# First layer of a two-block transformer kernel: own buffers for the squares, one sum each, queries in own banks, another split and order of the 31 conv taps

## The chip, the core and the metric

The kernel runs on one core of a Trainium2 chip. The metric is the time of one execution on the device in microseconds (us), the median of several runs. A core has TensorE (matrix products, into PSUM), VectorE, ScalarE and GpSimd (elementwise work) and SyncE, which here issues the transfers. Each engine works through its own queue in order; semaphores order the engines against each other.

## The reference

Two blocks of two layers each on 512 tokens of width 1,024, all in float32. What the change touches is the mixer of the first layer and the norms:

```python
def conformer_conv(u, b_glu, w_dw, b_dw, ln_g, ln_b):
    u = u + b_glu
    a, gate = jnp.split(u, 2, axis=-1)
    v = a * jax.nn.sigmoid(gate)
    v = causal_dwconv(v, w_dw, b_dw)          # 31 taps for each of 768 channels
    v = layernorm(v, ln_g, ln_b)
    return jax.nn.silu(v)

# layer 0 of first_block
mem_n = rmsnorm(mem, g_mem)                   # 256 tokens
h = rmsnorm(x, g_mix[0])
mem_k, mem_v = jnp.split(mem_n @ w_mem_kv[0], 2, axis=-1)
p = h @ w_in_a[0]
u, q_mem = p[..., :2 * CONV_CH], p[..., 2 * CONV_CH:]
mix = conformer_conv(u, ...)
mem_o = memory_attention(q_mem, mem_k, mem_v) # 4 heads of 64, 256 keys
x = x + jnp.concatenate([mix, mem_o], axis=-1) @ w_out[0]
x = x + conv_ffn(rmsnorm(x, g_ffn[0]), ...)
```

Layer 1 has forgetting attention in place of the conv; the second block has a gated MLP and grouped attention. Each rmsnorm or layernorm takes an inverse root per token.

## The kernel before

**Layout.** Channels lie on the 128 partitions, tokens along a row. x is 8 tiles of 128 x 512. Every product is made in three parts: x and the weights are split in a high part (ScalarE, xs_hi and w_hi) and the rest (xs_lo by VectorE, w_lo by GpSimd), and products (L1467 to L1471) adds hi x hi, lo x hi and hi x lo into a PSUM bank.

**Units.** The weights come as 128 x 1,024 units in one stream through four slots. SyncE loads a unit when GpSimd has made the low part of the one four before; high (L580) waits until TensorE has used that slot's unit. unit (L1473) is 24 products of 512 columns, one bank acc[a % 2], and waits until VectorE has read the bank two units back (acc_free). The first layer has four units on mem (keys and values, 256 columns), two for the queries of the memory attention (QM0), twelve GLU units (value and gate of six conv tiles in turn), four for layer 1's keys and values of mem (U_MEM1) and eight for the output.

**Norms.** ScalarE squares, VectorE adds the tiles (sq_sum, add_square L951), TensorE sums over channels into one column per 128 tokens (stat L1532, with mem, x and so on as names), VectorE makes the inverse root of that column by shift and three Newton steps (invert L961), TensorE spreads it over a bank (cast L1545) and VectorE copies it to SBUF (spread L992). The products do not wait for it; the results are scaled by it when they leave the bank (scaled L925, where GLU's pieces go to glu and gate). The squares have two buffers, so that a square waits for the addition two before it. There are 15 inverse roots in the kernel.

**Memory attention.** Eight blocks of two heads; a step (a_step L1700) is the scores of block i, the transposes of block i-1 and at two steps the output of four blocks. Between them: maximum (VectorE, maxima L1016), exponentials (ScalarE), reciprocal (VectorE, inverses L1028), scaling (GpSimd), transposes (TensorE), one copy each by VectorE (even_down L1036) and ScalarE. The steps stand at places given by a table of (GLU unit, chunk):

```python
A_AT = [divmod(2 + 5 * i, KT) for i in range(10)]
```

**Conv.** glu_product (L1154) makes a tile. Of its 31 taps VectorE does the first 15 (conv_taps L1162, two chains that are added at the end), TensorE the other 16 by products of 32 x 32 diagonals into four banks (conv_parts L1652), which ScalarE copies (parts_down) and TensorE folds into one bank (conv_fold L1670); conv_finish (L1148) adds it to VectorE's part. The diagonals are made by GpSimd (diagonals L535). VectorE's taps of tile t stand in the queue beside GLU units 2t+2 and 2t+3:

```python
if t >= 0:
    conv_taps(t, at, at + 2)
    at += 2
```

between maxima and inverses of each attention step, and the rest in one run ahead of the next scaled. The tile's layernorm then sums channels on TensorE (ln_sums), centres (layer_norm L1093), squares in the two buffers and sums again (ln_stat L1708, one column sums of each tile as its square is there).

## Time and profile before

| | |
|---|---|
| median of 3 runs | 1802.07 us (1799.18 to 1802.62) |
| profiled execution, its own time | 1801.85 us |
| its span | 1800.1 us |
| busy in the span | TensorE 1693.8, VectorE 886.1, ScalarE 739.4, GpSimd 721.1 us |
| chain that ended last | TensorE 82%, VectorE 12%, ScalarE 3% |
| TensorE's GLU0, GLU1 end, first product | 63.8, 70.1, 73.25 us |
| first conv_parts, GLU11 end, chunk 2 of the output | 112.31, 172.6, 219.14 us |
| weight high part, sigmoid, table load (ScalarE) | 1.05, 0.72, 1.28 us |

The span is the time from the first instruction to the last of one profiled execution; 1.75 us of its time lie around it. Busy times of TensorE are modelled ends of pipelined products, so that the distance from one start to the next tells more. The granted clock is given as a share of 2.4 GHz.

### The profile page before, as it was taken

Reading aid. Unit: us, or ns where it says so; the run is one execution under the profiler, and the core shown is the slowest. Engines: PE = TensorE matmul, PEld = TensorE weight load, DVE = VectorE, ACT = ScalarE, POOL = GpSimd, SP = SyncE. Lnnn points to the kernel's source line nnn. Section 1 sums busy time; section 2 is a strip of 40 time slices with the busy share of each in tenths; the row PEclk is TensorE's granted clock in tenths of the full one; section 3 lists DMA queues with packets and bytes.
Section 4 is the critical chain, followed back from the end, with each engine's and each line's share of the span. In section 5 each row is a group of like instructions: output and inputs, shape, how many; then the busy total and the mean of one; then the engine's idle time right before and its main releaser. Section 6 shows DMA issues by size and latency. Waiting matters only on the chain.

```text
span 1800.1 us, 23956 instructions
## 1 busy us (share of the span) xinstructions
PE 1693.8 (94%) x8636; PEld 1303.8 (72%) x8636; DVE 886.1 (49%) x1360; ACT 739.4 (41%) x1143; POOL 721.1 (40%) x409
## 2 busy tenths in 40 slices
PE   4989899999999999999999999998999997899995
PEld 4756778888888776677788888886776676676674
DVE  7588645554420035433556666102655455655444
ACT  5433343444432245444455555222327352327350
POOL 5433243444444434444344444543334332334340
PEclk9999899999999999999999999998999998999997
DMA  5211122222233222111222233332211112211111
GB/s 205 79 37 60 47 94 94 93 93 93 93 117 98 101 82 70 48 48 59 71 94 93 96 102 100 110 105 99 75 55 48 59 59 77 79 50 48 59 36 47
DMA packets 39818, 142.71 MB, mean 79 GB/s; under 512 B 4416, under 2 KB 4416, under 8 KB 39744
## 3 DMA queue, kind: packets, MB, share of 16 engines
q1 hardware_dynamic: 39024, 139.59, 23.6%
q10 hardware_dynamic: 720, 2.10, 0.3%
q8 instruction: 51, 0.84, 0.2%
q14 instruction: 23, 0.19, 0.0%
HBM read 139.57 MB, written 2.10 MB: 79 GB/s over the span
## 4 chain that ended last, share of the span: by engine, by line
PE 82%; DVE 12%; ACT 3%; issue 2%; DMA 0%; POOL 0%; SPq 0%; DVEq 0%; ACTq 0%; POOLq 0%
PE banks L1469 23%; PE banks L1470 23%; PE banks L1471 23%; PE banks L1573 3%; PE banks L1608 3%; PE banks L1591 2%; DVE chain L1170 2%; DVE sq_sum L959 1%; PE banks L1551 1%; PE banks L1664 1%; ACT prob L634 1%; PE banks L1823 1%; PE banks L1541 1%; DVE pt L1456 1%; DVE xs_lo L1326 1%
## 5 line engine op out<-in xcount | busy, mean ns | idle before, releaser
L507 POOL TENSOR_TENSOR w_lo<-raw,w_hi 128x1024 fp32r<-128x1024 f32 x255 | 625.2, 2461 | 822.5 <-ACT w_hi L586 822.3
L1469 PE MATMUL banks<-xs_hi,w_hi 128*128 128x512 f32 x1592 | 644.6, 405 | 28.0 <-DVE xs_lo L1326 12.8
L1471 PE MATMUL banks<-xs_hi,w_lo 128*128 128x512 f32 x1592 | 626.4, 393 | 0.0
L1470 PE MATMUL banks<-xs_lo,w_hi 128*128 128x512 f32 x1592 | 626.2, 393 | 0.0
L586 ACT ACTIVATE w_hi<-raw 128x1024 fp32r<-128x1024 f32 x255 | 263.6, 1051 | 300.0 <-PE banks L1471 292.1
L1469 PEld LDWEIGHTS banks<-xs_hi,w_hi 128*128 128x128 f32 x1592 | 302.7, 190 | 110.4 <-issue 39.3
L1471 PEld LDWEIGHTS banks<-xs_hi,w_lo 128*128 128x128 f32 x1592 | 302.5, 190 | 65.4
L1470 PEld LDWEIGHTS banks<-xs_lo,w_hi 128*128 128x128 f32 x1592 | 303.2, 190 | 59.4 <-issue 1.4
L517 POOL TENSOR_SCALAR prob<-prob,rinv 128x512 f32<-128x512 f32 (+3 forms) x144 | 87.2, 620 | 186.6 <-DVE rinv L1034 186.3
L634 ACT ACTIVATE prob<-banks,nmax 128x512 f32<-128x512 f32 (+3 forms) x144 | 83.3, 583 | 172.6 <-DVE nmax L1025 172.4
L1471 PE MATMUL banks<-hid_hi,w_lo 128*128 128x512 f32 x352 | 139.1, 395 | 0.0
L1469 PE MATMUL banks<-hid_hi,w_hi 128*128 128x512 f32 x352 | 139.0, 395 | 0.0
L1470 PE MATMUL banks<-hid_lo,w_hi 128*128 128x512 f32 x352 | 139.0, 395 | 0.0
L1025 DVE TENSOR_REDUCE nmax<-banks 128x2 f32<-128x1024 f32 (+3 forms) x72 | 69.9, 971 | 103.5 <-PE banks L1573 67.8
L1090 DVE TENSOR_TENSOR x<-x,banks 128x512 f32<-128x512 f32 x16 | 11.0, 688 | 203.8 <-PE banks L1471 203.8
L1071 DVE TENSOR_TENSOR u_v<-banks,rstd 128x512 f32<-128x512 f32 x44 | 30.5, 692 | 141.1 <-PE banks L1471 141.1
L676 ACT ACTIVATE t_v<-u_v,par 128x512 f32<-128x512 f32 x44 | 36.0, 817 | 116.2 <-DVE u_v L1071 116.2
L1471 PEld LDWEIGHTS banks<-hid_hi,w_lo 128*128 128x128 f32 x352 | 66.1, 188 | 16.1
L1469 PEld LDWEIGHTS banks<-hid_hi,w_hi 128*128 128x128 f32 x352 | 66.1, 188 | 16.1
L1470 PEld LDWEIGHTS banks<-hid_lo,w_hi 128*128 128x128 f32 x352 | 66.1, 188 | 15.9
L1591 PEld LDWEIGHTS banks<-cst,prob 128*128 128x128 f32 x440 | 47.4, 142 | 33.3 <-issue 28.6
L1170 DVE SCALAR_TENSOR_TENSOR chain<-glu,par,chain 128x512 f32<-128x512 f32 x78 | 65.2, 898 | 0.0
(205 smaller groups left out, 1741.0 us busy)
## 6 DMA issues: line engine op xcount, KB each, us to landing
raw<-wstream SPq DMA_DIRECT2D x255, 512.0 KB, 3.4
x<-xT SPq DMA_DIRECT2D x4, 512.0 KB, 10.8
out<-x SPq DMA_DIRECT2D x8, 256.0 KB, 2.0
memx<-memT SPq DMA_DIRECT2D x2, 512.0 KB, 6.3
ws_sb<-wsT ACTq DMA_DIRECT2D x2, 512.0 KB, 3.5
sb_sb<-sbT ACTq DMA_DIRECT2D x2, 256.0 KB, 4.0
rope_sb<-rope ACTq DMA_DIRECT2D x1, 512.0 KB, 5.0
par<-params SPq DMA_DIRECT2D x1, 338.5 KB, 3.9
```

The lines of the kernel that those rows point to most:

```text
L507: nc.gpsimd.tensor_tensor(w_lo[s][:].rearrange("p k c -> p (k c)"), raw[s][:], w_hi[s][:].rearrange("p k c -> p (k c)").bitcast(f32), SUB) ...
L517: nc.gpsimd.tensor_scalar(prob[b % 2][:, e, 0:nk], prob[b % 2][:, e, 0:nk], rinv[:, n:n + 1], 1.0, MUL, MUL).then_inc(at_p, 1)
L586: A(w_hi[s][:].rearrange("p k c -> p (k c)"), raw[s][:], ACT.Copy).then_inc(unit_hi, 1)
L634: A(prob[b % 2][:, e, 0:nk], a.s[b % len(a.s)][:, e, 0:nk], ACT.Exp, bias=nmax[:, n:n + 1], accum_out=rsum[:, n:n + 1]).then_inc(at_exp, 1)
L1025: V.tensor_reduce(nmax[:, n:n + 2], a.s[b % len(a.s)][:, :, 0:nk], AX.X, ALU.max, negate=True).then_inc(at_max, 1)
L1170: own.did(V.scalar_tensor_tensor(out=c, in0=window, scalar=weight, in1=c, op0=MUL, op1=ADD))
L1469: MM(dst, w_hi[slot][:, k, :], hi, start=start, stop=False)
L1470: MM(dst, w_hi[slot][:, k, :], lo, start=False, stop=False)
L1471: return MM(dst, w_lo[slot][:, k, :], hi, start=False, stop=stop)
L1573: last = MM(dst[:, e, 0:nk], a.q_of(h, qt), a.k_of(h, nk), start=True, stop=not a.causal)
L1591: last = nc.tensor.transpose(a.t[e][:, k * P:(k + 1) * P], prob[b % 2][:, e, k * P:(k + 1) * P], ident)
L1608: last = MM(a.o[n % len(a.o)][half(e), q0:T], a.v_of(2 * p + e, k), pt_of(a, p)[e][:, k, q0:T], start=(k == 0), stop=(k == nt - 1))
```

## The change

- The squares of mem and x go to buffers of 8 tiles each, mem_sq and x_sq, which lie where glu and conv come later. ScalarE no longer waits for VectorE between them, and VectorE makes each sum by one tensor_reduce over the 8 tiles (a step of 1 KB for mem, 2 KB for x between the numbers that are added). The order of ScalarE's queue at the start is another: the weight parts 1, 3, 4, 5 move, the last two behind all pairs of x. The halo of glu is cleared after the sums.
- The two query units write to banks 2 and 3. The x statistic moves from the first query unit to the second, the cast from there to GLU0's chunk 4; GLU0 and GLU1 don't wait for their banks; the value transposes come after GLU0 and GLU1.
- The attention's ten steps stand at 12 + 43 i / 9 chunks in place of 2 + 5 i: the first in GLU1, the last in GLU6. conv_parts and conv_fold begin one unit later and then run without a gap.
- Taps are dealt out one to a chunk, behind the attention's steps, where maxima, even_down and inverses now stand together. VectorE has 15 taps of tiles 0 to 4 and 7 of tile 5, TensorE 16 and 24.
- At the end: layer_norm comes before the low parts of the attention's output; its squares go to glu, without a wait; ln_stat runs ahead of the third mem unit, the cast ahead of the fourth; the last two mem results are scaled behind two of the tiles.
- In all 15 inverse roots two of the three temporaries lie in the PSUM bank of the sums, and a Newton step multiplies in another order, with as many instructions.

```diff
-PE_TAPS = 16
-DVE_TAPS = CW - PE_TAPS
+PE_TAPS = (16, 16, 16, 16, 16, 24)
+DVE_TAPS = tuple(CW - n for n in PE_TAPS)
-A_AT = [divmod(2 + 5 * i, KT) for i in range(10)]
+A_AT = [divmod(12 + 43 * i // 9, KT) for i in range(10)]
...
+        x_sq = put("x_sq", [P, KT, T], f32, squares_at)
+        mem_sq = put("mem_sq", [P, KT, TM], f32, squares_at + KT * T * 4)
...
                 A(mem_hi[:, k, :], memx[:, k, :], ACT.Copy, scale=col("g_mem", k)).then_inc(memsplit_hi, 1)
-            high(1)
+                if k == 3:
+                    high(1)
+            high(2)
             for k in range(KT):
-                if k >= 2:
-                    act.wait_ge(sq_added, norm_at["mem"][1] + k - 1)
-                A(sqm[k % 2][:], memx[:, k, :], ACT.Square).then_inc(squared, 1)
-            high(2)
+                A(mem_sq[:, k, :], memx[:, k, :], ACT.Square).then_inc(first_squared, 1)
...
-                square("x", k, x[:, k, :])
-                if k in (1, 4, 6):
-                    high(3 + (1, 4, 6).index(k))
+                A(x_sq[:, k, :], x[:, k, :], ACT.Square).then_inc(first_squared, 1)
+                if k == 1:
+                    high(3)
+            high(4)
+            high(5)
...
-                if t >= 2:
-                    act.wait_ge(ln_summed, t - 1)
-                A(sq[t % 2][:], conv[:, t, :], ACT.Square).then_inc(ln_squared, 1)
+                A(glu[:, t, 0:T], conv[:, t, :], ACT.Square).then_inc(ln_squared, 1)
...
-                m, r, t = small_m[:, 0:w], small[:, 0:w], small_t[:, 0:w]
+                m, t = (b_mix[:, TM + 64 * i:TM + 64 * i + w] for i in range(2))
+                r = small[:, 0:w]
...
-                    own.link(V.scalar_tensor_tensor(out=t, in0=r, scalar=-0.5, in1=r, op0=MUL, op1=MUL))
-                    own.link(V.tensor_tensor(t, t, m, MUL))
+                    own.link(V.tensor_tensor(t, m, r, MUL))
+                    own.link(V.scalar_tensor_tensor(out=t, in0=t, scalar=-0.5, in1=r, op0=MUL, op1=MUL))
...
+            dve.wait_ge(first_squared, KT)
+            V.tensor_reduce(sqm_sum[:], mem_sq[:].rearrange("p k t -> p t k"), AX.X, ADD).then_inc(first_summed, 1)
             for k in range(KT):
...
-                add_square("x", k)
-                if k == 3:
+                if k == 5:
                     invert("mem")
-                if k == 6:
-                    spread("mem", rstd_m, TM)
+            dve.wait_ge(first_squared, 2 * KT)
+            V.tensor_reduce(sq_sum[:], x_sq[:].rearrange("p k t -> p t k"), AX.X, ADD).then_inc(first_summed, 1)
+            spread("mem", rstd_m, TM)
...
             glu_product(MT - 1)
+            own.wait()
+            conv_taps(MT - 1, 0, DVE_TAPS[MT - 1])
             conv_finish(MT - 2)
+            conv_finish(MT - 1)
+            layer_norm("ln", (0,), conv, MT, bank[2])
...
-            unit(U_QM0, U_QM0, first=KT * SP_A, before=[(2, lambda: stat("x"))], wait_acc=False)
-            unit(U_QM0 + 1, U_QM0 + 1, before=[(2, lambda: cast("x"))], wait_acc=False)
-            pe.wait_ge(acc_free, U_QM0)
-            values_up(VT_M0, mem_kv0[:, 2, :], 2)
+            unit(U_QM0, U_QM0, first=KT * SP_A, wait_acc=False, dst=bank[2])
+            unit(U_QM0 + 1, U_QM0 + 1, before=[(2, lambda: stat("x"))], wait_acc=False, dst=bank[3])
...
+                if j == 0:
+                    before.append((4, lambda: cast("x")))
+                unit(U_GLU + j, U_GLU + j, before=before, freed=xs_free if j == 2 * MT - 1 else None, wait_acc=j >= 2)
...
+            ln_stat()
             mem_unit(U_MEM1 + 2, half_bank(acc[1], 0))
-            ln_stat()
+            cast("ln")
             mem_unit(U_MEM1 + 3, half_bank(acc[1], 1))
-            cast("ln")
```

Where instructions moved, by the order on three engines. Names: vm is the value copy of mem, prob the exponentials, gate the sigmoid's tile, raw and w_hi the weight units, chain the tap sums, nmax, rinv and pt0 the attention's maxima, reciprocals and transposed blocks.

ScalarE, from the first value copy to the second block of exponentials, before:

```order
L657 ACTIVATE vm0_95<-banks3 128x2x128 [waits vt_up]
L634 ACTIVATE prob0_68,rsum_79<-banks1,nmax_78 128x256 [waits at_max]
L634 ACTIVATE prob0_68,rsum_79<-banks1,nmax_78 128x256
L634 ACTIVATE prob1_69,rsum_79<-banks1,nmax_78 128x256 [waits at_max]
L634 ACTIVATE prob1_69,rsum_79<-banks1,nmax_78 128x256
L644 ACTIVATE pt0_1_97<-banks2 128x2x128 [waits at_t]
L586 ACTIVATE w_hi2_58<-raw2_54 128x1024 [waits unit_in2,unit_used]
L657 ACTIVATE vm0_95<-banks3 128x2x128 [waits vt_up]
```

and now:

```order
L661 ACTIVATE vm0_97<-banks3 128x2x128 [waits vt_up]
L590 ACTIVATE w_hi2_58<-raw2_54 128x1024 [waits unit_in2,unit_used]
L661 ACTIVATE vm0_97<-banks3 128x2x128 [waits vt_up]
L638 ACTIVATE prob0_68,rsum_79<-banks1,nmax_78 128x256 [waits at_max]
L638 ACTIVATE prob0_68,rsum_79<-banks1,nmax_78 128x256
L590 ACTIVATE w_hi3_59<-raw3_55 128x1024 [waits unit_in3,unit_used]
L734 ACT_TABLE_LOAD
L734 ACTIVATE gate0_106<-gate0_106,par_82 128x512 [waits acc_free]
L638 ACT_TABLE_LOAD
```

The second value copy stood behind the exponentials of blocks 0 and 1 and now stands ahead of the first; the weight part of unit 11 and the table load follow the first block's.

VectorE, from the product of tile 0 on, before:

```order
L1157 SCALAR_TENSOR_TENSOR glu_91<-glu_91,par_82,gate0_106 128x512 [waits gate_ok]
L1025 TENSOR_REDUCE nmax_78<-banks1 128x2 [waits at_exp,at_s,glu_ok]
L1167 TENSOR_SCALAR chain0_110<-glu_91,par_82 128x512
L1167 TENSOR_SCALAR chain1_111<-glu_91,par_82 128x512
L1034 RECIPROCAL rinv_80<-rsum_79 128x2 [waits at_p,at_exp]
L1043 COPY pt0_0_96<-banks2 128x2x128 [waits at_t]
L1025 TENSOR_REDUCE nmax_78<-banks1 128x2 [waits at_exp,at_s]
L1170 SCALAR_TENSOR_TENSOR chain0_110<-glu_91,par_82,chain0_110 128x512 [waits dve_did]
L1170 SCALAR_TENSOR_TENSOR chain1_111<-glu_91,par_82,chain1_111 128x512 [waits dve_did]
L1034 RECIPROCAL rinv_80<-rsum_79 128x2 [waits at_p,at_exp]
L1043 COPY pt0_0_96<-banks2 128x2x128 [waits at_t]
```

and now:

```order
L1154 SCALAR_TENSOR_TENSOR glu_91<-glu_91,par_82,gate0_106 128x512 [waits gate_ok]
L1027 TENSOR_REDUCE nmax_78<-banks1 128x2 [waits at_s,glu_ok]
L1045 COPY pt0_0_98<-banks2 128x2x128 [waits at_t]
L1036 RECIPROCAL rinv_80<-rsum_79 128x2 [waits at_exp]
L1164 TENSOR_SCALAR chain0_110<-glu_91,par_82 128x512
L1164 TENSOR_SCALAR chain1_111<-glu_91,par_82 128x512
L1167 SCALAR_TENSOR_TENSOR chain0_110<-glu_91,par_82,chain0_110 128x512 [waits dve_did]
L1167 SCALAR_TENSOR_TENSOR chain1_111<-glu_91,par_82,chain1_111 128x512 [waits dve_did]
L1167 SCALAR_TENSOR_TENSOR chain0_110<-glu_91,par_82,chain0_110 128x512 [waits dve_did]
L1027 TENSOR_REDUCE nmax_78<-banks1 128x2 [waits at_exp,at_s]
L1045 COPY pt0_0_98<-banks2 128x2x128 [waits at_t]
L1036 RECIPROCAL rinv_80<-rsum_79 128x2 [waits at_p,at_exp]
```

The taps stood between a maximum and its reciprocal; now the copy alone does, and the taps follow, three of them before the next maximum.

TensorE, at the end of the conv, from the channel sums on, before:

```order
L1705 MATMUL banks<-conv,cst 128x512 [waits conv_down]
L1705 MATMUL banks<-conv,cst 128x512 x4
L1705 MATMUL banks<-conv,cst 128x512 [waits conv_down]
L1469 MATMUL banks<-mem_hi,w_hi_56 128x256 [waits unit_lo]
L1470 MATMUL banks<-mem_lo,w_hi_56 128x256
L1471 MATMUL banks<-mem_hi,w_lo_60 128x256
```

and now:

```order
L1702 MATMUL banks<-conv,cst 128x512 [waits conv_down]
L1702 MATMUL banks<-conv,cst 128x512 x4
L1702 MATMUL banks<-conv,cst 128x512 [waits conv_down]
L1710 MATMUL banks<-cst,glu 128x1 [waits ln_squared,stat_inv]
L1710 MATMUL banks<-cst,glu 128x1 x3
```

A mem unit of 24 products stood behind the channel sums, and the sums of squares (cst and glu in the new rows) follow now at once.

## Rows read from the trace of the kernel before

**Rows 1.** The view by stretches: busy us (and count) of each engine, granted clock, DMA share, GB/s.
```profile
33.00:36.00 3.00, 2.92 (x9) 2.54 (x10) 3.00 (x6) 1.68 (x3) 0.03 (x1) 0.50 0.20 82
180.00:225.00 45.00, 39.57 (x254) 31.52 (x241) 30.35 (x53) 17.02 (x25) 11.18 (x3) 0.81 0.14 47
225.00:1800.00 1575.00, 1506.33 (x7080) 1167.55 (x7078) 720.43 (x1107) 648.47 (x985) 635.48 (x358) 0.98 0.24 78
```

**Rows 2.** The chain of work that ended last, 45 to 50 us: start, us, what.
```profile
47.59 0.23 PE banks L1469
```

**Rows 3.** Timeline, start of the kernel: start, us, engine, line, what, [idle before, releaser].
```profile
18.64 2.35 POOL L507 TENSOR_TENSOR w_lo<-raw,w_hi 128x1024 fp32r<-128x1024 f32 x1 [4.27 <-ACT w_hi L586]
...
20.21 0.61 ACT L607 ACTIVATE t_v<-x 128x512 f32<-128x512 f32 x1
...
33.08 1.23 PE L1551 MATMUL banks<-cst,small 128*128 128x128 f32 x4 [5.14 <-DVE small L987]
...
41.08 1.86 PE L1541 MATMUL banks<-cst,sq_sum 128*128 128x1 f32 x8 [4.37 <-DVE sq_sum L959]
```

**Rows 4.** VectorE's groups by line and shape: busy us, mean ns, idle before.
```profile
L1025 DVE TENSOR_REDUCE nmax<-banks 128x2 f32<-128x1024 f32 x38 | 46.4, 1222 | 55.9 <-PE banks L1573 44.7 <-PE banks L1582 11.1
```

**Rows 5.** Timeline of VectorE, first attention step and first product.
```profile
57.65 0.69 DVE L1025 TENSOR_REDUCE nmax<-banks 128x2 f32<-128x512 f32 x1 [1.59 <-PE banks L1573]
...
59.43 0.17 DVE L1034 RECIPROCAL rinv<-rsum 128x2 f32<-128x2 f32 x1 [1.09 <-ACT prob L634]
...
73.25 0.96 DVE L1157 SCALAR_TENSOR_TENSOR glu<-glu,par,gate 128x512 f32<-128x512 f32 x1 [2.44 <-ACT gate L729]
```

**Rows 6.** Timelines of VectorE and GpSimd: taps, and a fold, beside low parts.
```profile
79.14 5.19 DVE L1170 SCALAR_TENSOR_TENSOR chain<-glu,par,chain 128x512 f32<-128x512 f32 x4
...
80.33 2.79 POOL L507 TENSOR_TENSOR w_lo<-raw,w_hi 128x1024 fp32r<-128x1024 f32 x1
...
130.89 2.85 POOL L507 TENSOR_TENSOR w_lo<-raw,w_hi 128x1024 fp32r<-128x1024 f32 x1
...
131.61 0.75 DVE L1151 SCALAR_TENSOR_TENSOR conv<-banks,par,conv 128x512 f32<-128x512 f32 x1
```

**Rows 7.** Timeline of TensorE: the eighth score, the first conv_parts.
```profile
98.13 1.22 PE L1573 MATMUL banks<-mem_kv,qm 64*128 64x256 f32 x4 [5.79 <-ACT prob L634]
...
112.31 4.45 PE L1664 MATMUL banks<-glu,diag 32*32 32x512 f32 x128
```

**Rows 8.** Timelines of TensorE and VectorE, end of the first layer's conv.
```profile
172.63 1.06 PE L1676 MATMUL banks<-part,cst 128*32 128x512 f32 x8
...
182.81 8.69 DVE L1170 SCALAR_TENSOR_TENSOR chain<-glu,par,chain 128x512 f32<-128x512 f32 x13
...
195.19 2.08 PE L1705 MATMUL banks<-conv,cst 128*128 128x512 f32 x2 [4.45 <-DVE conv L1151]
...
201.34 0.95 PE L1713 MATMUL banks<-cst,t_g 128*128 128x1 f32 x8
...
214.34 1.05 PE L1551 MATMUL banks<-cst,small 128*128 128x128 f32 x8
...
219.14 0.50 PE L1469 MATMUL banks<-xs_hi,w_hi 128*128 128x512 f32 x1 [0.98 <-DVE xs_lo L1228]
```

**Rows 9.** Timelines of GpSimd, VectorE and TensorE, the inverse root pre0.
```profile
1267.76 7.18 POOL L507 TENSOR_TENSOR w_lo<-raw,w_hi 128x1024 fp32r<-128x1024 f32 x3 [25.02 <-ACT w_hi L586]
...
1270.03 0.16 DVE L979 TENSOR_SCALAR small_m<-banks 128x4 f32<-128x4 f32 x1 [2.05 <-PE banks L1541]
1270.22 2.40 DVE L981 TENSOR_SCALAR small_t<-small_m 128x4 int32<-128x4 int32 x1
...
1276.78 1.16 PE L1551 MATMUL banks<-cst,small 128*128 128x128 f32 x8 [2.56 <-DVE small L987]
```

**Rows 10.** Timeline of TensorE, the casts of f1 and fin.
```profile
887.77 1.16 PE L1551 MATMUL banks<-cst,small 128*128 128x128 f32 x8 [1.10 <-DVE small L987]
...
1249.02 2.08 PE L1551 MATMUL banks<-cst,small 128*128 128x128 f32 x8 [2.43 <-DVE small L987]
```

More of the change, by code:

```diff
@@ L230, in two_blocks @@
         gate = [take(f"gate{i}", [P, T]) for i in range(2)]
-        diag = [take(f"diag{i}", [P, PE_TAPS, Q]) for i in range(2)]
+        diag = [take(f"diag{i}", [P, max(PE_TAPS), Q]) for i in range(2)]
         chain = [take(f"chain{i}", [P, T]) for i in range(2)]
@@ L1141, in _ @@
                 mem_down(mem_kv0, j, U_MEM0, bank[4 + j // 2])
+            dve.wait_ge(first_summed, 2)
+            for t in range(MT):
+                own.did(V.memset(glu[:, t, 0:CW - 1], 0.0))
             invert("x")
@@ L1161, in conv_taps @@
             def conv_taps(t, first, end):
-                for tap in range(first, min(end, DVE_TAPS)):
+                for tap in range(first, min(end, DVE_TAPS[t])):
                     c = chain[tap % 2][:]
```

115 lines of the change are left out of this document (49 added, 66 removed).

## The prediction

> **What bounds the kernel now.** I read the view by stretches first. TensorE is close to full from 225 us to the end; the first layer, up to 225 us, is where it idles and where its clock falls: from 180 to 225 us it is busy 39.6 of 45 us at a granted clock of 0.81, and after a long idle time the clock reads 0.50, half of 2.4 GHz [rows 1]. At full clock a 512-column product starts every 0.23 us [rows 2], so a weight unit of 24 costs 5.6 us, and one on 256 columns 2.8.
>
> Then the timeline and what ended each idle time. At the start TensorE waits 5.14 us for the inverse root of mem and 4.37 us for the last partial sum of squares of x: ScalarE, VectorE and the two square buffers pass the turn around [rows 3]. In the middle it waits 5.79 us at the eighth score of the memory attention, since the maximum before it stands in VectorE's queue behind the taps of tile 0 [rows 7]. From 112.31 us, the first conv_parts, it is nearly never idle: five conv_parts (4.45 each), five folds (1.06) and six units fill the time to 173.7. At the end of the layer it waits 4.45 us for tile 5, whose 13 later taps and product run alone on VectorE, and then goes at a low clock through one-column sums that alternate with squares in two buffers [rows 8].
>
> Beyond 225 us only the inverse root changes. Where GpSimd makes low parts, VectorE's SBUF-only steps stand still: at pre0 the root takes 1270.03 to 1276.7, with 2.40 us on one four-element shift, and TensorE idles 2.56 us [rows 9]. Undisturbed its 12 steps take 2.4 us, and idle TensorE by 2.43 us at fin; at f1 the idle time is 1.10 [rows 10].
>
> **Part 1, the start.** Squares go to own buffers, so ScalarE no longer waits: a pair (high part, square) takes 0.61 + 0.52 = 1.13 us [rows 3], and 8 pairs and a weight unit end at about 27 us instead of 37. Behind them stand two high parts that were ahead of the last pairs before, so unit 4 (first query) gets its low part (2.35, [rows 3]) at about 31 instead of 34 us. The sum of x is one reduction of 4,096 elements. The nearest row has 1,024 elements in 1.22 us [rows 4]; less 0.15 fixed, that is 1.04 ns each, hence 4.4 us (mem: 2.3). These rows read neighbouring elements and the new one jumps 2 KB, so I bound it at 4.4 to 18 us and take 4.4, the row. It ends at about 36 us; behind it follow rstd_m, four copies and six memsets, to 38. The statistic of x now stands in the second query unit, which TensorE reaches at 39 to 40 us: no wait. Its cast moves into the first GLU unit, ending near 48; the queries have own banks, so units need not wait. Unit GLU1 ends near 58 (before: 70.1).
>
> But ScalarE's second value copy stands ahead of the first exponentials and waits for GLU1 and the transposes behind it. So exp 0, the gate, its sigmoid with the table load, and only then the first product follow: exp 1.1, scaled gate 0.7, weight part 1.0, table 1.28, sigmoid 0.7. First product at 62.8 us, before 73.25 [rows 5]: 10.4 us won, of which the idle gaps of about 2 us and a half-clock spell like that of [rows 1] make 3 uncertain.
>
> **Part 2, VectorE from the first product to the first conv_parts.** Before, the attention began in GLU0 and three of its steps lay where VectorE was idle. Now only the first does. Instructions between these points:
> full-width operations: before 27 taps + 1 sum + 2 products + 3 scaled + 2 query copies + 5 maxima = 40; now 37 + 2 + 3 + 4 + 2 + 7 = 55. At 0.63 us (0.67 for a tap, [rows 8]; 0.6 start to start for the others) 25.2 and 34.7. Half-width copies and reciprocals: 2.6 and 3.5. That gives 27.8 of the 39.1 us that rows 5 and 7 span, so 11.3 us were waits and blocked time. Now:
> each of 7 steps waits for its exponentials (1.09 us, [rows 5]) with only a 0.4 us copy in the gap, where two taps stood: 7 x 0.7 = 4.9; two sigmoids, 2.7 where exp, weight part and table load precede it and 0.8: 3.5. Blocked by GpSimd: four taps took 5.19 us, 2.5 more than 4 x 0.67, while a low part ran [rows 6]. Three low parts x 2.3, seven scalings x 0.4, one low part that mostly lies under a sigmoid wait 0.9: 10.6. Sum 38.2 + 4.9 + 3.5 + 10.6 = 57.2 us, between 50 (taps and scalings fit beside each other) and 62 (a low part hits every step).
> The first conv_parts thus starts at 62.8 + 57.2 = 120.0, one GLU unit further than at 112.31 before. It also waits for the second query copy, which stands behind seven taps of tile 2. From here TensorE is the bound again: five conv_parts, five folds and five units are 22.3 + 5.1 + 28 = 55.3, so the middle ends at 175.3 us, against 173.7 (172.63 + 1.06, [rows 8]): **+1.6**. So the ten microseconds of the start are eaten by VectorE, in the middle.
>
> **Part 3, the end of the layer**, counted from that end F. Before, the third chunk of the first output pair starts at 219.14 = F + 45.4 [rows 8]. Now:
> wait for the gate and mem unit 0.7 + 2.8 = 3.5; conv_parts of 24 taps 4.45 x 1.5 = 6.7, to 10.2; mem unit 2.8, to 13.0; fold 1.1, to 14.1. Tile 5 has 7 taps on VectorE (4.2), a product, a sum, two finishes and two low parts' blocking: ready at F + 10.5, no longer late. Six channel sums of 0.9 (2.08 for one at half clock, [rows 8]), to 19.6. Centring and first square 1.4, then 6 x 0.95 of one-column sums [rows 8], now back to back without buffer waits, to 26.7; part of them at half clock +1.2, to 27.9. Mem unit 2.8 to 5.1 by the clock, take 4.0, over the inverse root (2.6, hidden): 31.9. Cast 1.05, [rows 8], 32.9. Mem unit again 3.9, 36.8. Twelve products of chunks 0 and 1, 2.8: 39.6. VectorE reaches chunk 2 at cast + 5.0 (it waits for the mem unit in between), so it is hidden by 1 us. F + 39.6 against F + 45.4: **-5.8** (-3 to -8, all of it the clock in these short stretches).
>
> **Part 4, the inverse roots.** The temporaries move to PSUM, so each step reads at most one SBUF tensor. A step of that form (fold bank, conv) took its plain 0.75 us inside a GpSimd low part [rows 6], and the first step, PSUM to SBUF, took 0.16 us inside three low parts while the next, SBUF to SBUF, took 2.40 [rows 9]. So the roots no longer stall: pre0 and pre1 end before TensorE reaches the cast, -2.56 each, f1 -1.10, together **-6.2**; at f0, b nobody waited. Roots at fin, post0 and post1 were never blocked and are exposed. Writes to PSUM appear in no row; reading from it costs nothing extra (0.16, [rows 9]), so I price a step as now, bounds -0.3 to +0.8 us for each of three roots.
> The Trainium skill, "VectorE: DVE Perf Modes", section on the TRN2 errata, gives a PSUM source 120 fixed cycles against 58 for SBUF. By that rule 12 steps would cost 0.8 us more, 2.3 us for the three exposed roots, and the forecast would be 1794; the four-element read of PSUM does not show it.
>
> **Sum**: 1.6 - 5.8 - 6.2 = -10.4. The profiled execution took 1801.85 us, 0.2 under the median of 1802.07; on the median, 1791.7 us.
>
> **Rivals.**
> A, the start's gain survives: VectorE's stretch takes 50 us or less, so the first conv_parts begins at 113 or earlier and the middle gains 6 us: 1784. For it: VectorE had 11.3 us of waits before, and single taps between steps could fill some. Against: the steps stand as max, copy, reciprocal with nothing between.
> B, the attention is worse than counted: the new dealing puts every score behind its exponentials, GpSimd's scalings and the tap at hand, TensorE falls to half clock in gaps of over 4 us (as at 33 us, [rows 1]), and the middle ends 6 us later: 1798.
> C, the root's steps stay blocked, because their results still go to SBUF: no gain in part 4, 1798. The row of 0.75 us speaks against it.
> D, slower than before: the reduction with 2 KB jumps. If an element costs four times 1.04 ns, mem's sum takes 8.9 us and x's 17.7. VectorE ends x's sum near 52 instead of 36; 3.6 us of this are slack at the statistic, 12 us are not, TensorE idles over 4 us and takes 1.5 us more at half clock, and the first product slips to 76: 1791.7 + 13.5 = 1805. It decides from about 3.8 times the price; at twice, 1794.5. For it: no row reads such jumps. Against: no VectorE row with another pattern is slow.
> The Trainium skill, "SBUF — State Buffer", section "Door 1: The DMA port swizzle", says that SBUF has 16-byte lines and that each access to a new line pays a penalty, which here would be every element; it gives no size, and no row here shows it.
>
> **How the numbers follow.** Forecast, 1786 to 1797: 0.55. A 0.16, B 0.12, C 0.07, D 0.10. Likeliest time 1791.7. The range leaves out D and the tail of A and B: 1783 to 1799. About 0.2% (3.6 us) is what a measurement can tell from no change, so faster means under 1798.5: forecast and A, half of B and C: 0.80. Same: the other half and mild cases of D: 0.12. Slower: 0.08.
>
> **What would show it.** Start: TensorE's wait for the x sum gone, GLU1 ending near 58, the two reductions at 2.3 and 4.4 us. Middle: first product near 63, first conv_parts near 120, reciprocals with about 0.7 us idle ahead of each. End: no wait for tile 5, chunk 2 at F + 40. Later: roots of 2.4 us everywhere, no idle time ahead of the casts of f1, pre0, pre1. The forecast fails first if the stretch of part 2 is not 57 us, or if a reduction is much over 4.4.

## The result, and the profile after

The changed kernel takes 1790.6 us (median of 6 runs, 1790.0 to 1794.8) where the kernel before takes 1801.9 in the same session: ratio 0.995, 95% interval 0.9938 to 0.9961. The forecast was 1791.7 us. Its profiled execution has a span of 1791.2 us (before 1800.1).

A table of landmarks tells where the time went; later kernels stand in it too. "Middle end" is the end of the fifth fold, F in the prediction; "residual" the start of VectorE's first x = x + bank of the first layer.

| kernel | first product | first conv_parts | middle end | residual | median | ratio to before (95%) |
|---|---|---|---|---|---|---|
| before | 73.25 | 112.31 | 173.7 | 227.04 | 1801.9 | |
| changed | 63.87 | 118.76 | 175.2 | 224.66 | 1790.6 | 0.9950 (0.9938 to 0.9961) |
| x2, before with new roots | 73.23 | 112.45 | 173.8 | 226.99 | 1794.5 | 0.9953 (0.9936 to 0.9970) |
| x1, changed with old roots | 74.04 | 129.04 | 185.6 | 234.98 | 1808.8 | 1.0042 (1.0025 to 1.0059) |
| x9, x1 with mem's root earlier | 68.19 | 123.11 | 179.6 | 229.00 | 1803.4 | 1.0029 (1.0014 to 1.0043) |
| x7, additions for the x sum | 72.58 | 127.53 | 184.0 | 233.40 | 1801.2, one run | |
| x3, tap between | 63.54 | 115.99 | 174.1 | 221.92 | 1791.6 | 0.9949 (0.9933 to 0.9966) |
| x5, tile 0 with 7 taps | 64.61 | 113.72 | 172.3 | 220.04 | 1788.1 | 0.9931 (0.9914 to 0.9947) |
| x8, second value copy later | 64.97 | 119.48 | 176.0 | 227.04 | 1791.3 | 0.9955 (0.9939 to 0.9972) |
| x6, tile 5 with 15 taps | 64.23 | 119.04 | 175.1 | 234.32 | 1802.0 | 1.0016 (1.0002 to 1.0029) |
| x10, old order at the end | 63.06 | 118.00 | 174.5 | 220.28 | 1788.5 | 0.9947 (0.9928 to 0.9965) |
| b3, four edits | 64.81 | 114.99 | 173.7 | 222.49 | 1788.0 | 0.9941 (0.9927 to 0.9956) |
| b4, x5 and x10 together | 63.45 | 112.55 | 171.2 | 215.42 | 1784.6 | 0.9914 (0.9901 to 0.9928) |

Each ratio is against runs of before in the same session (medians 1799.8 to 1801.9), so the ratios compare better than the medians. The landmarks come from one profiled execution of each kernel and scatter: up to the middle's end x6 and x10 run the changed kernel's instructions, and their first products stand 1.2 us apart, their middle ends 0.6. The executions differ too: that of the changed kernel took 1793.0 us, 2.4 over its median, and that of x10 1784.9, 3.5 under its own.

The first layer is only 2.4 us shorter at the residual, and 6.5 of the 8.9 us between the two spans come after it. The residual's distance to the end scatters as well: 1562.1 to 1568.0 us with the new roots, 1572.7 to 1575.0 with the old (before, x1, x9). The timeline of VectorE in the changed kernel, at its start (start, us, engine, line, what, [idle before, releaser]); it answers to [rows 3, 5]:

```profile
18.17 3.89 DVE L1118 TENSOR_REDUCE sqm_sum<-mem_sq 128x256 f32<-128x2048 f32 x1 [2.31 <-ACT mem_sq L703]
...
33.47 7.56 DVE L1126 TENSOR_REDUCE sq_sum<-x_sq 128x512 f32<-128x4096 f32 x1
...
60.89 0.17 DVE L1036 RECIPROCAL rinv<-rsum 128x2 f32<-128x2 f32 x1 [3.78 <-ACT prob L638]
...
63.87 1.12 DVE L1154 SCALAR_TENSOR_TENSOR glu<-glu,par,gate 128x512 f32<-128x512 f32 x1 [2.23 <-ACT gate L734]
...
71.86 0.17 DVE L1036 RECIPROCAL rinv<-rsum 128x2 f32<-128x2 f32 x1 [0.76 <-ACT prob L638]
```

Less the same fixed 0.15 us, the sums take 1.8 ns an element, not 1.04, and the reciprocal of each of the seven later steps waits 0.76 us. TensorE's timeline of the same kernel, from the x statistic to the output (before: [rows 3, 7, 8]):

```profile
41.16 0.97 PE L1538 MATMUL banks<-cst,sq_sum 128*128 128x1 f32 x8
...
48.91 1.05 PE L1548 MATMUL banks<-cst,small 128*128 128x128 f32 x8
...
118.76 4.46 PE L1661 MATMUL banks<-glu,diag 32*32 32x512 f32 x128 [1.19 <-issue]
...
174.18 1.07 PE L1673 MATMUL banks<-part,cst 128*32 128x512 f32 x8
178.22 6.58 PE L1661 MATMUL banks<-glu,diag 32*32 32x512 f32 x192
...
188.81 5.42 PE L1702 MATMUL banks<-conv,cst 128*128 128x512 f32 x12
...
195.77 8.59 PE L1710 MATMUL banks<-cst,glu 128*128 128x1 f32 x48 [1.54 <-ACT glu L768]
...
208.80 1.05 PE L1548 MATMUL banks<-cst,small 128*128 128x128 f32 x8
...
214.15 0.47 PE L1462 MATMUL banks<-xs_hi,w_hi 128*128 128x512 f32 x1 [1.44 <-DVE mem_kv L1132]
...
216.97 0.39 PE L1462 MATMUL banks<-xs_hi,w_hi 128*128 128x512 f32 x1
```

The x statistic has no idle time ahead of it, and neither have the channel sums (L1702), that of tile 5 included. New are the 8.59 us of one-column sums in one run, and a wait of 1.44 us for the banks of the last mem results, ahead of the output's first product. Chunk 2 starts at 216.97 (before 219.14).

The roots, in the changed kernel: GpSimd and VectorE at pre0, answering to [rows 9]:

```profile
1264.47 7.16 POOL L511 TENSOR_TENSOR w_lo<-raw,w_hi 128x1024 fp32r<-128x1024 f32 x3 [25.50 <-ACT w_hi L590]
...
1266.73 0.17 DVE L981 TENSOR_SCALAR banks<-banks 128x4 f32<-128x4 f32 x1 [2.04 <-PE banks L1538]
1266.93 0.17 DVE L983 TENSOR_SCALAR banks<-banks 128x4 int32<-128x4 int32 x1
...
1268.95 0.16 DVE L989 SCALAR_TENSOR_TENSOR small<-banks,small 128x4 f32<-128x4 f32 x1
```

Twelve steps in 2.4 us, in the middle of three low parts, and TensorE's cast at 1270.76 has no wait. Its waits for roots beyond 225 us, from the view of waits (engine, line, waited for, us in total, times, longest), in the kernel before:

```profile
PE banks L1551 <- DVE small L987: 13.5, 6, 2.6
```

and in the changed kernel:

```profile
PE banks L1548 <- DVE small L989: 7.4, 3, 2.5
```

### The profile page after: what moved, and what is told of

It is laid out like the page before. It is cut to its first block, busy times and chain, and to the rows that moved or that the text cites. A ratio compares the mean times of both kernels' runs of the same rounds, so it can differ in the third digit from the quotient of the medians.

```text
span 1791.2 us, 24042 instructions
## 1 busy us (share of the span) xinstructions
PE 1697.3 (95%) x8700; PEld 1307.6 (73%) x8700; DVE 859.8 (48%) x1338; ACT 737.0 (41%) x1143; POOL 719.6 (40%) x409
## 4 chain that ended last, share of the span: by engine, by line
PE 84%; DVE 9%; ACT 3%; issue 2%; DMA 1%; POOL 1%; SPq 0%; DVEq 0%; ACTq 0%; POOLq 0%
PE banks L1462 24%; PE banks L1464 23%; PE banks L1463 23%; PE banks L1570 3%; PE banks L1605 3%; PE banks L1588 2%; DVE chain L1167 2%; PE banks L1661 1%; ACT prob L638 1%; PE banks L1548 1%; PE banks L1817 1%; DVE nmax L1027 1%; DVE pt L1449 1%; PE banks L1538 1%; DMA raw<-wstream 1%
## 5 line engine op out<-in xcount | busy, mean ns | idle before, releaser
L511 POOL TENSOR_TENSOR w_lo<-raw,w_hi 128x1024 fp32r<-128x1024 f32 x255 | 618.8, 2436 | 806.9 <-ACT w_hi L590 806.6
L521 POOL TENSOR_SCALAR prob<-prob,rinv 128x512 f32<-128x512 f32 (+3 forms) x144 | 92.4, 654 | 193.3 <-DVE rinv L1036 193.0
L1588 PE MATMUL banks<-cst,prob 128*128 128x128 f32 x440 | 65.5, 283 | 5.2 <-POOL prob L521 5.2
```

The source lines that it names most:

```text
L511: nc.gpsimd.tensor_tensor(w_lo[s][:].rearrange("p k c -> p (k c)"), raw[s][:], w_hi[s][:].rearrange("p k c -> p (k c)").bitcast(f32), SUB) ...
L521: nc.gpsimd.tensor_scalar(prob[b % 2][:, e, 0:nk], prob[b % 2][:, e, 0:nk], rinv[:, n:n + 1], 1.0, MUL, MUL).then_inc(at_p, 1)
L1588: last = nc.tensor.transpose(a.t[e][:, k * P:(k + 1) * P], prob[b % 2][:, e, k * P:(k + 1) * P], ident)
```

## The experiments

### The roots: x2, x1 and x9

**x2** is the kernel before with this edit alone:

```diff
-                m, r, t = small_m[:, 0:w], small[:, 0:w], small_t[:, 0:w]
+                m, t = (b_mix[:, TM + 64 * i:TM + 64 * i + w] for i in range(2))
+                r = small[:, 0:w]
...
-                    own.link(V.scalar_tensor_tensor(out=t, in0=r, scalar=-0.5, in1=r, op0=MUL, op1=MUL))
-                    own.link(V.tensor_tensor(t, t, m, MUL))
+                    own.link(V.tensor_tensor(t, m, r, MUL))
+                    own.link(V.scalar_tensor_tensor(out=t, in0=t, scalar=-0.5, in1=r, op0=MUL, op1=MUL))
```

> The kernel before with only the new inverse roots (temporaries in PSUM). Theory: the idle time ahead of the casts of f1, pre0 and pre1 goes, the wait of 5.1 us at mem's cast shrinks only where a low part hit that root; time 1801.9 - 6.2 = 1795.7 us, up to 2 us lower if mem's root was hit too. The rest of the change (first layer) then accounts for no more than 5 us. Rival, the gain needs the new first layer: less than 3 us, 1799 or more.

Measured 1794.5 against 1801.5 us: -7.0, near the theory's number. Its residual stands at 226.99, where it stood before, so all of it is beyond the first layer. **x1** is the changed kernel with the same lines put back.

> The changed kernel with only the inverse roots put back (temporaries in SBUF, old order of the Newton step). Theory: the SBUF-only steps stand still while GpSimd makes low parts, so TensorE idles again ahead of the casts of f1 (1.1 us), pre0 and pre1 (2.6 each); the waits at fin, post0 and post1 stay at 2.4 to 2.5; time 1790.6 + 6.2 = 1796.8 us. Rival 1, the roots brought little and the rest comes from elsewhere: 1791 to 1793. Rival 2, a step with PSUM operands costs more, hidden so far in the three exposed roots: their waits fall by 0.2 us or more each and the time is 1795 or less.

Measured 1808.8 us: 18 more than the changed kernel, and slower than before. Both rivals and the theory's number fall. The later part is near what was foretold: TensorE waits 15.2 us for roots beyond 230 us, 7.8 more than in the changed kernel, of 6.2 forecast. The other 10 us are in the first layer, at mem's root, which the prediction never priced in its new place. VectorE, GpSimd and TensorE of x1:

```profile
28.25 0.16 DVE L987 TENSOR_TENSOR small_t<-small_t,small_m 128x2 f32<-128x2 f32 x1
28.45 2.34 DVE L988 SCALAR_TENSOR_TENSOR small<-small_t,small 128x2 f32<-128x2 f32 x1
30.82 0.97 DVE L986 SCALAR_TENSOR_TENSOR small_t<-small 128x2 f32<-128x2 f32 x1
31.83 2.27 DVE L987 TENSOR_TENSOR small_t<-small_t,small_m 128x2 f32<-128x2 f32 x1
34.13 0.97 DVE L988 SCALAR_TENSOR_TENSOR small<-small_t,small 128x2 f32<-128x2 f32 x1
...
28.43 2.35 POOL L511 TENSOR_TENSOR w_lo<-raw,w_hi 128x1024 fp32r<-128x1024 f32 x1 [5.33 <-ACT w_hi L590]
30.74 1.04 POOL L543 TENSOR_TENSOR diag<-cst,par 128x512 f32<-128x512 f32 x1
31.75 2.33 POOL L511 TENSOR_TENSOR w_lo<-raw,w_hi 128x1024 fp32r<-128x1024 f32 x1
34.04 1.04 POOL L543 TENSOR_TENSOR diag<-cst,par 128x512 f32<-128x512 f32 x1
...
35.16 1.22 PE L1547 MATMUL banks<-cst,small 128*128 128x128 f32 x4 [6.53 <-DVE small L988]
```

Each of the last four steps lasts about as long as the GpSimd instruction beside it (2.34 beside 2.35, 0.97 beside 1.04). **x9** moves mem's root out of that spell, by 0.7 us:

```diff
-                if k == 5:
+                if k == 4:
                     invert("mem")
```

> The kernel with the old roots in the changed first layer (it took 1808.8 us), with one more edit: the root of mem stands behind the fifth low part of x and not behind the sixth, 0.7 us earlier in VectorE's queue, so that its twelve steps of 0.2 us end at about 28.4 us, as GpSimd's low parts begin. Theory (the 18 us between the old and the new roots are 8 us at later roots, and 10 us because four steps of mem's root fell among low parts that begin at 28.4): the root takes 2.4 instead of 8.2 us, the cast's wait falls from 6.5 to about 2 us, the x sum ends near 41 instead of 48, and the time is 1798 to 1800 us. Rival (the old roots cost the first layer 10 us for another reason, the order of the Newton step or the place of the temporaries): 1806 to 1809 us, with mem's root still 4 us or longer.

1803.4 us: 5.4 less than x1, of 9 to 11 expected. The cause is right: the root is undisturbed and TensorE's cast has no wait; the size isn't, since VectorE's three last low parts of x still stand behind GpSimd, the x sum ends at 42.5 instead of 41.0, TensorE waits 4.89 us for it and comes out slower, with the cast of x at 53.2 instead of 48.9. From the residual on, x9 is 6.2 us longer than the changed kernel (1572.7 to 1566.5 us to the end of the span): the term of part 4. The new root changes two things, where its temporaries lie and the order of a step's products; no run separates them, so what is shown is that the two together escape GpSimd.

### The reduction: x4 and x7

**x4** puts ten instructions behind mem's results, such as

```diff
+            probe(V.tensor_reduce(o, flat[:, 0:1024].rearrange("p (t k) -> p t k", k=8), AX.X, ADD))
+            probe(V.tensor_reduce(o, flat[:, 0:2048].rearrange("p (t k s) -> p t k s", k=8, s=2)[:, :, :, 0], AX.X, ADD))
+            probe(V.tensor_reduce(o, x_sq[:, :, 0:128].rearrange("p k t -> p t k"), AX.X, ADD))
```

> The changed kernel with ten extra VectorE instructions behind the scaled keys and values of mem, which read x_sq and write a scratch row that nothing uses: sums of 8 numbers for 128 results, the numbers 4, 8, 16, 64 bytes, 2 KB (every second result), 2 KB, 1 KB (sums of 4, 256 results) and 1 KB apart, one over 4,096 neighbouring numbers, and one addition of two tiles. Time itself is of no interest (some 15 us longer). Theory (the price is in the jump from one number to the next): 1,024 neighbouring numbers take 1.2 us and 4,096 4.4, as the maxima do, and 1 KB and 2 KB jumps take 1.9 to 2.0 us for 1,024. Rival 1 (any jump over 16 bytes costs the same): 64 bytes takes 1.9 us too, 8 bytes 1.2. Rival 2 (it isn't the jump but a sum of 8 numbers for each result, or a read from SBUF): the neighbouring ones take 1.9 and 7.6 us as well.

The expectation names one of them wrongly: the sums of 4 (256 results) take one number from each of four tiles, and these lie 2 KB apart, not 1 KB. VectorE's timeline; the rows are jumps of 4, 8, 16, 64 bytes (256 numbers only), 2 KB three times (L1144 to L1146), 1 KB, and 4,096 neighbours:

```profile
41.86 1.21 DVE L1140 TENSOR_REDUCE chain<-x_sq 128x128 f32<-128x1024 f32 x1
43.10 1.22 DVE L1141 TENSOR_REDUCE chain<-x_sq 128x128 f32<-128x1024 f32 x1
44.35 1.99 DVE L1142 TENSOR_REDUCE chain<-x_sq 128x128 f32<-128x1024 f32 x1
46.38 0.58 DVE L1143 TENSOR_REDUCE chain<-x_sq 128x32 f32<-128x256 f32 x1
47.00 2.03 DVE L1144 TENSOR_REDUCE chain<-x_sq 128x128 f32<-128x1024 f32 x1
49.06 1.94 DVE L1145 TENSOR_REDUCE chain<-x_sq 128x128 f32<-128x1024 f32 x1
51.03 1.89 DVE L1146 TENSOR_REDUCE chain<-x_sq 128x256 f32<-128x1024 f32 x1
52.95 1.87 DVE L1147 TENSOR_REDUCE chain<-x_sq 128x128 f32<-128x1024 f32 x1
54.86 4.42 DVE L1148 TENSOR_REDUCE chain<-x_sq 128x512 f32<-128x4096 f32 x1
```

The price is in the jump, but it comes in one step, at 16 bytes, and doesn't grow beyond: 4 and 8 bytes cost 1.04 ns a number (less 0.15 us for the instruction), 16 bytes and everything above 1.7 to 1.8. So theory and rival 1 hold together (the edge lies at 16 bytes, not above), rival 2 falls. **x7** makes the x sum by additions:

```diff
-            V.tensor_reduce(sq_sum[:], x_sq[:].rearrange("p k t -> p t k"), AX.X, ADD).then_inc(first_summed, 1)
+            own.link(V.tensor_tensor(sq_sum[:], x_sq[:, 0, :], x_sq[:, 1, :], ADD))
+            for k in range(2, KT - 1):
+                own.link(V.tensor_tensor(sq_sum[:], sq_sum[:], x_sq[:, k, :], ADD))
+            V.tensor_tensor(sq_sum[:], sq_sum[:], x_sq[:, KT - 1, :], ADD).then_inc(first_summed, 1)
```

> The changed kernel with the x sum made by seven additions of two tiles (512 neighbouring numbers each) from the large buffers, instead of one reduction over 2 KB jumps that took 7.56 us. Theory: seven additions of 0.6 to 0.7 us, 4.3 to 4.9 us, so the sum ends 2.7 to 3.2 us earlier, but TensorE reaches the statistic at about 41 us in both, so the first product stays within 1 us of 63.9 and the time within 1.5 us of 1790.6. Rival (the reduction was late and held the statistic, the cast and the queries up): first product 2 to 3 us earlier, time 1788.

Both are wrong: the single run took 1801.2 us, 10.6 more than the changed kernel; TensorE waits 8.90 us at the statistic. VectorE and GpSimd of x7:

```profile
32.81 2.88 DVE L1126 TENSOR_TENSOR sq_sum<-x_sq 128x512 f32<-128x512 f32 x1
35.73 10.42 DVE L1128 TENSOR_TENSOR sq_sum<-sq_sum,x_sq 128x512 f32<-128x512 f32 x5
46.18 0.69 DVE L1129 TENSOR_TENSOR sq_sum<-sq_sum,x_sq 128x512 f32<-128x512 f32 x1
...
36.57 8.31 POOL L511 TENSOR_TENSOR w_lo<-raw,w_hi 128x1024 fp32r<-128x1024 f32 x3
```

Five additions take 10.42 us beside three low parts, where one takes 0.69 alone, while the reduction took 7.3 to 7.6 us in every kernel here beside such low parts. The slower instruction is the better one, because it isn't stopped. The additions bring nearly what rival D feared of the reduction: a first product at 72.58, where D had 76.

### The middle: x3, x5 and x8

**x3**, in each attention step:

```diff
+                        if t >= 0:
+                            conv_taps(t, at, at + 1)
                         if i < att_m0.n:
                             inverses(att_m0, i)
...
-                    if t >= 0:
+                    if t >= 0 and not a_steps(j, k):
                         conv_taps(t, at, at + 1)
```

> The changed kernel, but in each attention step the one tap of that chunk stands between the copy and the reciprocal, not behind the reciprocal. Nothing else moves. Theory (VectorE is the bound from the first product at 63.9 to the first conv_parts at 118.8 us, and the 0.76 us that it waits for the exponentials in each of seven steps lie on the path): the idle time ahead of the reciprocals goes, the first conv_parts starts 3 to 5 us earlier, near 115, and the time is 1786 to 1788 us. Rival 1 (TensorE's or GpSimd's turn binds there: the scalings wait 0.7 us longer for the reciprocal only where a tap is slow): first conv_parts within 1 us of 118.8, time 1790 to 1791. Rival 2 (a tap hit by GpSimd delays reciprocal, scaling and transposes): conv_parts 1 to 3 us later, 1792.

First conv_parts 2.8 us earlier, so rival 1 falls at the landmark, but the theory's time isn't reached: 1791.6 us. The idle time ahead of five of the reciprocals is gone, yet the first conv_parts itself took longer (4.46 in the changed kernel, behind 1.19 us of idle time):

```profile
115.99 6.06 PE L1663 MATMUL banks<-glu,diag 32*32 32x512 f32 x128 [1.84 <-issue]
```

The granted clock reads 1.00 from 113 to 116 us, in a stretch with 1.84 us of idle time, then 0.52 to 119 us and 0.92 to 122; in the changed kernel it is 1.00 throughout. At the middle's end 1.1 us are left, little more than the scatter, and the median shows no gain. **x5** takes work away from VectorE:

```diff
-PE_TAPS = (16, 16, 16, 16, 16, 24)
+PE_TAPS = (24, 16, 16, 16, 16, 24)
```

> The changed kernel with 7 taps of tile 0 on VectorE instead of 15 (TensorE 24). VectorE has eight taps less between the first product and the first conv_parts (8 x 0.67 = 5.4 us and what GpSimd blocks), TensorE has 2.2 us more in that conv_parts. Theory (VectorE binds this stretch): its end, 118.8 us, moves 4 to 6 us earlier, the middle ends 2 to 3 us earlier, time 1787 to 1789 us. Rival 1 (TensorE's own work and its half clock bind once the waits go): conv_parts 1 to 3 us earlier, the middle ends where it did or 1 us earlier, time 1790 to 1792. Rival 2 (nothing in front of conv_parts hangs on VectorE): conv_parts at 118.8, time 1793.

First conv_parts 5.0 us earlier, middle end 2.9, time 1788.1: the theory in all three numbers. The landmarks are clear of the scatter, the time less so: the interval of its ratio overlaps that of the changed kernel. So VectorE is what binds from the first product to the first conv_parts. **x8** puts ScalarE's second value copy behind the exponentials:

```diff
-                if j < 2:
+                if j == 0:
                     mem_values_down(j)
...
+                if j == 1:
+                    mem_values_down(j)
```

> The changed kernel with ScalarE's second value copy behind the first block's exponentials. In the changed kernel it stands ahead and waits for GLU1 and the transposes, so the exponentials start at 59.8 though their maximum is there at 57.1. Theory (this order holds up VectorE's reciprocal, gate and the first product): exponentials at 57.2, first product at 62 to 62.5 instead of 63.9, first conv_parts 1 to 2 us earlier than 118.8, time 1789 to 1790.5 us. Rival (GLU1's end at 59.1 and the sigmoid's table load bind anyway): first product within 0.5 us of 63.9, time 1790.6.

Open in the sum, settled in the piece: from the cast of x to the first product it is 14.06 us (50.91 to 64.97) where it was 14.96, and each distance comes back within 0.01 us in the other kernels with the same order (14.06 in b3). So the order costs 0.9 us, half of what I expected. But in x8 the cast itself came 2.0 us later, TensorE having waited 2.34 us at the statistic and then run slower, ahead of anything that the edit moved, and the time is that of the changed kernel.

### The end: x6 and x10

**x6** sets PE_TAPS of tile 5 back to 16.

> The changed kernel with the old split for tile 5: 15 taps on VectorE, 16 on TensorE. Theory (in this place VectorE is the late one): TensorE's conv_parts of tile 5 takes 4.5 instead of 6.6 us, but VectorE, now 8 taps (5.4 us and more beside GpSimd) later, lets the channel sum of tile 5 wait 4 to 5 us, as in the kernel before; the end of the layer comes 2 to 4 us later, time 1793 to 1795. Rival (there is slack, or the idle time only replaces work): within 1 us of the changed kernel, 1790 to 1791.5.

1802.0 us: 11 more, not 2 to 4. TensorE's fold of tile 5, VectorE's taps and GpSimd's low part in x6:

```profile
193.97 1.93 PE L1673 MATMUL banks<-part,cst 128*32 128x512 f32 x8 [8.34 <-DVE conv L1148]
...
179.37 10.83 DVE L1167 SCALAR_TENSOR_TENSOR chain<-glu,par,chain 128x512 f32<-128x512 f32 x13
190.23 2.71 DVE L1170 TENSOR_TENSOR conv<-chain,chain 128x512 f32<-128x512 f32 x1
193.07 0.75 DVE L1148 SCALAR_TENSOR_TENSOR conv<-banks,par,conv 128x512 f32<-128x512 f32 x1
...
186.80 5.59 POOL L511 TENSOR_TENSOR w_lo<-raw,w_hi 128x1024 fp32r<-128x1024 f32 x1 [5.11 <-ACT w_hi L590]
```

Two things that I left out: the change puts tile 4's finish behind tile 5's taps, and the fold of tile 5 needs the bank that this finish frees; and VectorE and GpSimd hold each other up: the low part that starts among the taps takes 5.59 us instead of 2.35, and the addition behind the taps 2.71 instead of 0.69. With 7 taps the finish comes in time (VectorE at 185.89, the fold at 187.82) and GpSimd's next low part (189.06, 2.35 us) starts behind them. **x10** keeps the 7 taps and undoes the order behind the channel sums. The squares go to two buffers again, too, and both last mem results are scaled ahead of the spread of the root, so that x10 tests these three together:

```diff
-            ln_stat()
             mem_unit(U_MEM1 + 2, half_bank(acc[1], 0))
-            cast("ln")
+            ln_stat()
             mem_unit(U_MEM1 + 3, half_bank(acc[1], 1))
+            cast("ln")
```

> The changed kernel with the old order after the channel sums: the third mem unit ahead of the sums of squares, these alternating with squares in two buffers, the fourth mem unit ahead of the cast, both mem results scaled ahead of the spread. The 7 taps of tile 5 and everything ahead stay. Theory (the term of 5.8 us for the end is more than tile 5's taps: half clock, turns between the engines and TensorE's idle time at the output also count): the first residual comes 2 to 3 us later than 224.7, time 1792.5 to 1794. Rival (the end gains by the taps of tile 5 alone; the one-column sums take 8 us in either order): first residual within 1 us of 224.7, time 1790 to 1791.5.

The theory is wrong in its sign. The residual comes 45.8 us after the middle's end, in the changed kernel 49.4: the old order is 3.6 us shorter. The table bears out the sign: this distance is 47.7 to 51.0 us in the eight kernels with the new order and 7 taps, 45.8 and 44.2 in the two with the old. TensorE's one-column sums, first and last, and the output in x10:

```profile
196.13 0.95 PE L1712 MATMUL banks<-cst,t_g 128*128 128x1 f32 x8
...
200.62 1.54 PE L1712 MATMUL banks<-cst,t_v 128*128 128x1 f32 x8
...
212.33 0.50 PE L1464 MATMUL banks<-xs_hi,w_hi 128*128 128x512 f32 x1 [1.02 <-DVE xs_lo L1223]
```

Behind a mem unit the sums take 6.0 us at a granted clock of 0.90, in front of it 8.59 at 0.61, and the wait of 1.44 us for the mem banks goes. By the measured time the gain is not certain: ratio 0.9947 beside 0.9950, though the medians differ by 2.1 us.

### What beats both: b3 and b4

b3 joins x3, x5 and x8, and scales the last mem results behind one tile instead of two.

> The changed kernel with four edits: the tap between copy and reciprocal (alone: first conv_parts 2.8 us earlier, time 1791.6), 7 taps of tile 0 on VectorE (alone: 1788.1), ScalarE's second value copy behind the first exponentials, and the last two mem results scaled behind one normalised tile instead of two. Theory (VectorE binds from the first product to the first conv_parts, in series, so that the gains add): first product near 62.5, first conv_parts at 109 to 111 us, middle end 3 to 5 us earlier than the changed kernel's 175.2, time 1785 to 1788 us. Rival (TensorE's own work is the bound once 5 us are gone): no earlier than with the 7 taps alone, first conv_parts 113 to 114, time 1787.5 to 1789.

1788.0 us, the rival: from first product to first conv_parts it needs 50.2 us, x5 alone 49.1 (from the cast of x 64.2 and 64.1), so that the tap between brings nothing more once VectorE has less to do. b4 joins x5 and x10.

> The changed kernel with the two edits that moved most alone: 7 taps of tile 0 on VectorE (first conv_parts 5.0 us earlier) and the old order after the channel sums (alone: the first residual came 45.8 us after the middle's end, in the changed kernel 49.5). Theory (both stretches are in series and what they give adds): first conv_parts near 114, middle end 172 to 173, first residual 218 to 219 us against 224.7, time 1784 to 1787 us. Rival (the one takes the other's: which of the short stretches runs at half clock depends on where idle time falls, so that the end is no shorter than 48 us once it comes earlier): first residual 220.5 to 222, time 1787.5 to 1790.

1784.6 us, ratio 0.9914: middle end 171.2, residual 215.42 (44.2 after it). At the residual the gains add (4.6 and 4.4 us alone, 9.2 together), and b4 is faster than the changed kernel by more than the intervals.

## Why the prediction was right, point by point

**The sum** was -10.4 us and the medians moved by -11.3. Between the two spans it is -8.9, and by parts:

| part | forecast | spans |
|---|---|---|
| 1 and 2, middle end | +1.6 | +1.6 |
| 3, the end of the layer | -5.8 | -3.9 at the residual |
| 4, the roots | -6.2 | -6.5 for all beyond the residual |

**Part 1** was right in its result (63.87 for 62.8) and wrong in a term: the reduction of x took 7.56 us, not 4.4, mem's 3.89 for 2.3. I had taken the maxima's price of neighbouring numbers [rows 4]; the jumps cost 1.75 times that (x4). Rival D was the right mechanism at a size far below its point of four times. The sum ended at 41.0 instead of 36, and the statistic, which I had reached at 39 to 40, came at 41.16 without idle time; in every other kernel with this start and the new roots (x3, x4, x5, x6, x8, x10, b3, b4) TensorE waits 1.0 to 2.7 us there. "No wait" came true in this execution only because TensorE was late itself. The view by stretches, 30 to 41 us, in the changed kernel and in x5, and x5's statistic:

```profile
30.00:41.00 11.00, 10.24 (x34) 8.01 (x34) 11.00 (x4) 3.44 (x7) 11.00 (x6) 0.69 0.42 105
...
30.00:41.00 11.00, 7.98 (x38) 6.40 (x38) 10.97 (x6) 2.24 (x3) 11.00 (x7) 1.00 0.43 128
...
40.16 1.05 PE L1538 MATMUL banks<-cst,sq_sum 128*128 128x1 f32 x8 [2.70 <-DVE sq_sum L1126]
```

At a granted clock of 0.69 it filled the time in which it waits 2.70 us at 1.00. So the mis-sized reduction does bind; that the landmark came within 1.1 us of the forecast is in part luck.

The prediction's prices for D don't follow from its own premise either: at 4 x 1.04 ns and 0.15 us the sums take 8.7 and 17.2 us, not 8.9 and 17.7, and a straight line between its two points (1794.5 at twice, 1805 at four times) crosses 1798.5 at 2.8 times and the median of before at 3.4, not 3.8.

The Trainium skill, "SBUF — State Buffer", section "Door 1: The DMA port swizzle", gives 16-byte lines and a penalty for each new line; x4 agrees with the line and adds its size, 0.6 to 0.8 ns for a float. It also says that four floats of stride are free, and there the measurement differs: a jump of 16 bytes already took 1.99 us for 1.22.

**Part 2.** The stretch took 54.9 us for 57.2, with the waits of 0.76 us that were forecast as 0.7, and x5 shows that VectorE is its bound. The gain of 9.4 us at the first product is lost there, as forecast. That the middle's end came within 0.1 us of the forecast is luck: the first product was 1.1 us late, the stretch 2.3 us short, and the rest took 56.5 us for 55.3. Not foreseen was how little a shorter stretch returns: x3 gave back 1.6 of its 2.8 us in a conv_parts at a clock of 0.72.

**Part 3** named the right cause, tile 5, for a sum that was 2 us too good. Chunk 2 stands at F + 41.7, forecast F + 39.6. The step "6 x 0.95, plus 1.2 at half clock" took 8.59 for 6.9 us (7.3 to 9.6 in the others with this order). And the step "VectorE reaches chunk 2 at cast + 5.0, hidden by 1 us" missed what is needed before chunk 0: TensorE waits for the banks of the mem results, which stand in VectorE's queue behind two normalised tiles, and these took 3.05 us beside a low part. Nor did I price the order by itself: in x10 its undoing, with the buffers and the place of the mem results, shortens the end by 3.6 us, where the changed kernel is 3.9 us shorter than before. So the gain comes from what x10 keeps, the 7 taps of tile 5 above all (x6), against the order; the 7 taps alone in the kernel before were not run.

**Part 4.** f1, pre0 and pre1 lost their waits, fin, post0 and post1 kept 2.5 us each. Counted from the residual to VectorE's copies of the spread roots, the changed kernel gains 1.4 us at f1, 2.8 more at pre0 and 2.7 more at pre1, and gives back 0.5 in between: 6.4. A step on PSUM takes 0.16 to 0.17 us, as on SBUF, so that neither bound of it was needed. The Trainium skill gives a PSUM source 120 fixed cycles against 58 for SBUF ("VectorE: DVE Perf Modes", section on the TRN2 errata); that difference shows in no step here.

The mistake that didn't cost me: I added the parts as if they were independent. The new start puts the end of mem's root among GpSimd's low parts, and only the new form of the root runs on there. Alone, the new roots give -7.0 us; alone, the rest of the change gives +7.3 (x1 against 1801.5); together they give -11.3. A forecast for the first layer's part alone, made the same way, would have read -4.2 and been wrong by over 11 us.

**Rivals.** A didn't happen (the stretch was 54.9, not under 50), nor B (middle end within 0.1 us of the forecast). C was tested by the rows of pre0: steps that write to SBUF with an operand in PSUM aren't stopped. D is above.

## What to carry to other kernels

Before an instruction of VectorE moves to another time, look what GpSimd does at that time, and whether the instruction is of the kind that is stopped: a root of 2.4 us took 8.2 (x1), and a part of a change can be worth more than the whole. Judge an order at the end of a stage by what the first consumer needs first, bank included, and test it apart from the work that was taken out with it. And a few microseconds won ahead of TensorE's next stretch came back only in part where that stretch then ran at a lower clock (x3).
